# Sums that end token half by token half, a shorter root, and a norm folded into the next one's weights

## The reference

```python
def rms_norm(x, g):
    y = xf * lax.rsqrt(jnp.mean(xf * xf, axis=-1, keepdims=True) + RMS_EPS)
    return (y * g.astype(jnp.float32)).astype(x.dtype)
def swiglu(x, w_gu, w_down):
    gate, up = jnp.split(x @ w_gu, 2, axis=-1)
    return (jax.nn.silu(gate) * up) @ w_down
# first_block
    h = h + merged @ w_out[l]                                  # stage "out"
    h = h + peer(rmsnorm(h, norm2_w[l]), ...)                  # "wq", "pu", "pv"
    return rmsnorm(h, final_norm_w)
# second_block
    x = x + 0.5 * rms_norm(swiglu(rms_norm(x, ffn1_pre_g[l]), ...), ffn1_post_g[l])   # "gu1", "dn1"
    y = hybrid_mixer(rms_norm(x, mix_pre_g[l]), ...)                                  # "in2" ... "wo"
    x = x + rms_norm(y, mix_post_g[l])
    x = x + 0.5 * rms_norm(swiglu(rms_norm(x, ffn2_pre_g[l]), ...), ffn2_post_g[l])   # "gu2", "dn2"
```

## Time and profile before

| | us |
|---|---|
| median of 3 runs | 1586.11 (1584.76 to 1589.0) |
| profiled execution | 1585.57 |
| its span | 1584.0 |
| TensorE busy, matmul | 1502.1 (95%) |
| VectorE busy | 1117.8 (71%) |
| ScalarE busy | 732.2 (46%) |
| GpSimd busy | 272.1 (17%) |

### The profile page before, as it was taken

How to read it: one execution, slowest core, us unless ns; L and a number is a source line. 1 busy time by engine, 2 the same in 40 slices (tenths; PEclk the granted TensorE clock), 3 DMA queues, 4 the chain that set the end, 5 groups by cost and what they waited for, 6 DMA issues and landing times.

```text
span 1584.0 us, 27622 instructions
## 1 busy us (share of the span) xinstructions
PE 1502.1 (95%) x10710; PEld 1381.2 (87%) x10710; DVE 1117.8 (71%) x1590; ACT 732.2 (46%) x835; POOL 272.1 (17%) x306
## 2 busy tenths in 40 slices
PE   7999998999999999999999999989999886699997
PEld 7989897999999999998888888879998785599975
DVE  5557666699999898657676676667773665677743
ACT  4356653545454444444444444444433455244431
POOL 1100000000000111136556545500000100000000
PEclk9999999999999999999999999999999995899999
DMA  7643334476665877788888877745555440335551
GB/s 256 217 160 135 130 141 166 154 246 233 238 230 206 279 262 267 250 306 293 289 304 279 287 291 297 284 146 194 204 185 185 135 173 1 133 137 209 187 184 53
DMA packets 56291, 329.66 MB, mean 208 GB/s; under 512 B 7472, under 2 KB 7520, under 8 KB 24720
## 3 DMA queue, kind: packets, MB, share of 16 engines
q1 hardware_dynamic: 35856, 259.01, 46.2%
q0 software_dynamic: 20352, 69.47, 12.7%
HBM read 294.90 MB, written 33.55 MB: 207 GB/s over the span
## 4 chain that ended last, share of the span: by engine, by line
PE 84%; DVE 10%; ACT 4%; DMA 1%; issue 1%; DVEq 0%; SPq 0%; ACTq 0%
PE ub L1535 14%; PE ub L1536 14%; PE ub L1537 14%; PE acc L1535 11%; PE acc L1537 11%; PE acc L1536 11%; DVE wl L878 3%; PE acc L1729 3%; DMA raw<-in_wstream 1%; ACT wh L528 1%; PE acc L1600 1%; PE mb L1625 1%; PE acc L1499 1%; PE mb L1610 0%; DVE esel L1231 0%
## 5 line engine op out<-in xcount | busy, mean ns | idle before, releaser
L878 DVE TENSOR_TENSOR wl<-raw,wh 128x2048 fp32r<-128x2048 f32 x245 | 582.6, 2379 | 300.2 <-ACT wh L528 298.9
L1535 PE MATMUL ub<-xh,wh 128*128 128x256 f32 x2216 | 622.5, 281 | 6.6 <-DVE wl L878 5.8
L528 ACT CAST wh<-raw 128x2048 fp32r<-128x2048 f32 x245 | 467.9, 1910 | 337.0 <-DMA raw<-in_wstream 239.7
L1536 PE MATMUL ub<-xl,wh 128*128 128x256 f32 x2216 | 615.3, 278 | 0.0
L1537 PE MATMUL ub<-xh,wl 128*128 128x256 f32 x2216 | 615.2, 278 | 0.0
L1535 PEld LDWEIGHTS ub<-xh,wh 128*128 128x128 f32 x2216 | 417.3, 188 | 13.7 <-DVE wl L878 7.1
L1536 PEld LDWEIGHTS ub<-xl,wh 128*128 128x128 f32 x2216 | 418.1, 189 | 0.1
L1537 PEld LDWEIGHTS ub<-xh,wl 128*128 128x128 f32 x2216 | 418.1, 189 | 0.0
L1535 PE MATMUL acc<-wh,ah 128*128 128x512 f32 x512 | 199.2, 389 | 0.5 <-issue 0.5
L1537 PE MATMUL acc<-wh,al 128*128 128x512 f32 x512 | 199.2, 389 | 0.0
L1536 PE MATMUL acc<-wl,ah 128*128 128x512 f32 x512 | 199.2, 389 | 0.0
(11 more groups left out here) (309 smaller groups left out, 1641.4 us busy)
## 6 DMA issues: line engine op xcount, KB each, us to landing
raw<-in_wstream SPq DMA_DIRECT2D x245, 1024.0 KB, 4.9
gates<-gst POOLq DMA_DIRECT2D x16, 1024.0 KB, 15.4
gl_in<-gates POOLq DMA_DIRECT2D x64, 256.0 KB, 4.9
hidden<-hid POOLq DMA_DIRECT2D x60, 256.0 KB, 5.1
hid<-hidden POOLq DMA_DIRECT2D x60, 256.0 KB, 4.8
resid<-in_x SPq DMA_DIRECT2D x2, 512.0 KB, 3.9
rb<-in_rel POOLq DMA_DIRECT2D x1, 1024.0 KB, 8.1
wb<-in_ffn_post_g POOLq DMA_DIRECT2D x2, 512.0 KB, 3.8
```

The source lines that it names most:

```text
L528: act.copy(wh[:, slot, :], raw[:, slot % RAW, :]).then_inc(w_high, 1)
L878: v.tensor_tensor(wl[:, slot, :], raw[:, slot % RAW, :], wh[:, slot, :].bitcast(F32), ALU.subtract).then_inc(w_low, 1)
L1535: pe.matmul(dst, sh, mh, start=first, stop=False)
L1536: pe.matmul(dst, sh, ml, start=False, stop=False)
```

## The change

1. In the five acc stages the last two chunks are one tail (`acc_tail`): its matmuls go bank by bank, 12 each, for both chunks. The semaphore `a_half` rises after token half 0 and again after bank 2, `c_done` by two at the end. The tail starts when both chunks, and in `pv` both steps' `al`, are there. Additions, squares and roots go by half 0, bank 2 and bank 3. The preparation of the chunk that `ahead` gave after the last chunk of an acc stage is moved behind `normed` of the next stage.
2. The root has two steps in place of three: after the first guess 7 instructions stood for 9, with constants that give the root times a factor `ROOT`, which the mean's factor takes out again. A factor of 0.5 or 1-LAM_INIT goes into the mean as well.
3. After `pv` the transposes take the bare sum. `final_norm_w` is multiplied into the columns of the next norm's weights (`fcol`), `y_again` holds `resid * wb`, and both means and roots are computed together on four columns (`two_roots`). `resid` is scaled after unit 0 (`first_scaled`).
4. The row for the scaling is made between the two tiles of unit 1 (`split_unit`), no longer ahead of it. Transposed blocks lie in `mb`, `ub` and the banks 0 and 1 of `acc`.
5. The output leaves in three copies. `shift_y`, a tile without use, is 8 columns smaller and `fcol` takes that place.

```diff
-            return (acc[:, k, 0:T] if k < 4 else mb[:, k - 4, 0:T] if k < 6 else
-                    ub[:, 1 - u % 2, (k - 6) * T:(k - 5) * T])
+            bank = (mb[:, 0, :], mb[:, 1, :], ub[:, 1 - u % 2, :], acc[:, 0, :], acc[:, 1, :])
+            at = k % 2 * T if k >= 2 else 0
+            return bank[k if k < 2 else k // 2 + 1][:, at:at + T]
...
-            for tt in range(TT):
-                sp.wait_ge(r_ok, LAST_R + tt + 1)
-                sp.dma_start(out[tt * P:tt * P + P, :], resid[:, tt, :]).then_inc(x_out, 16)
+            for n, (tt, lo, hi) in enumerate(((0, 0, D), (1, 0, HALF), (1, HALF, D))):
+                sp.wait_ge(r_ok, R_OF["dn2"] + n + 1)
+                sp.dma_start(out[tt * P:tt * P + P, lo:hi], resid[:, tt, lo:hi]).then_inc(x_out, 16)
...
+            pool.dma_start(fcol[:, :], A["fcol"]).then_inc(par1, 16)
...
-            def square_acc(scratch):
-
-                square(acc_of(0), scratch, 0)
-                halves[0] += 1
-                act.wait_ge(half_ok, halves[0])
-                square(acc_of(1), scratch, 1)
+            def square_acc(stage, scratch):
+
+                h = 2 * TAILS.index(stage)
+                act.wait_ge(a_half, h + 1)
+                square(acc_of(0), scratch, 0)
+                act.wait_ge(a_half, h + 2)
+                square(acc[:, 2, :], scratch, 1)
+                act.wait_ge(c_done, CH[stage] + dict(_sizes)[stage])
+                square(acc[:, 3, :], scratch, 2)
...
                 normed(w, UN[gu])
-                square_resid(junk_again, 1)
+                square_resid(stage, 1, junk_again)
+                if stage == "pv":
+                    act.wait_ge(t_ok, 2)
+                    square(y_again[:, 1, :], junk_again, 3, ROOT / 32.0)
                 C, U = CH[gu], UN[gu]
+                ahead(C - 1)
...
-                for _ in range(3):
-                    link(v.tensor_tensor(ta, dst, dst, ALU.mult))
-                    link(v.scalar_tensor_tensor(tb, ta, -0.5, src, ALU.mult, ALU.mult))
-                    link(v.scalar_tensor_tensor(dst, tb, 1.5, dst, ALU.add, ALU.mult))
+                guess(dst, src, ti)
+                link(v.tensor_tensor(tb, dst, dst, ALU.mult))
+                link(v.tensor_tensor(ta, tb, src, ALU.mult))
+                link(v.scalar_tensor_tensor(tb, ta, 10.0 / 3.0, ta, ALU.subtract, ALU.mult))
+                link(v.scalar_tensor_tensor(dst, tb, 5.0, dst, ALU.add, ALU.mult))
+                link(v.tensor_tensor(tb, dst, dst, ALU.mult))
+                link(v.tensor_tensor(ta, tb, src, ALU.mult))
+                link(v.scalar_tensor_tensor(dst, ta, 64.0 / 3.0, dst, ALU.subtract, ALU.mult))
+
+            def root(lo, hi):
...
+                    for t in range(lo, hi):
+                        x, z = var[:, t:t + 1], rstd[:, t:t + 1]
+                        ins = v.scalar_tensor_tensor(nw_a[:, t:t + 1], z, x, z, ALU.mult, ALU.mult)
+                    link(ins)
...
-                v.wait_ge(c_done, CH[stage] + dict(_sizes)[stage])
-                weighted(scratch)
-                if factor != 1.0:
-                    link(v.tensor_scalar(rstd[:, :], rstd[:, :], factor, None, ALU.mult))
-                for tt in range(TT):
-                    next_resid(v.scalar_tensor_tensor(resid[:, tt, :], scratch[:, tt, :], rstd[:, tt:tt + 1],
-                                                      resid[:, tt, :], ALU.mult, ALU.add))
+                weights()
+                squares(1)
+                link(v.tensor_tensor(scratch[:, 0, :], acc_of(0), wb[:, :], ALU.mult))
+                mean(0, 1, factor=factor)
+                root(0, 1)
+                squares(1)
+                v.tensor_tensor(scratch[:, 1, half(0)], acc[:, 2, :], wb[:, half(0)], ALU.mult)
+                next_resid(v.scalar_tensor_tensor(resid[:, 0, :], scratch[:, 0, :], rstd[:, 0:1],
+                                                  resid[:, 0, :], ALU.mult, ALU.add))
+                squares(1)
+                v.tensor_tensor(scratch[:, 1, half(1)], acc[:, 3, :], wb[:, half(1)], ALU.mult).then_inc(wb_used, 1)
+                both_halves()
+                mean(1, 2, factor=factor)
+                root(1, 2)
+                for n in range(2):
+                    next_resid(v.scalar_tensor_tensor(resid[:, 1, half(n)], scratch[:, 1, half(n)], rstd[:, 1:2],
+                                                      resid[:, 1, half(n)], ALU.mult, ALU.add))
...
+            add_first("out")
+            add_half("out", 0)
+            squares(1)
+            mean(0, 1)
+            root(0, 1)
+            add_half("out", 1)
+            v.tensor_scalar(y[:, 0, :], resid[:, 0, :], rstd[:, 0:1], None, ALU.mult).then_inc(t_in, 1)
...
-            add_acc("pv")
-            rstd_ready()
...
+            def first_norm():
+
+                add_first("pv")
+                weights()
+                v.wait_ge(r_ok, nr[0])
+                weigh(0)
+                add_half("pv", 0)
+                add_half("pv", 1)
+
+            def two_roots():
+
+                v.wait_ge(r_ok, nr[0])
+                weigh(1)
+                v.engine_nop().then_inc(wb_used, 1)
+                squares(4)
+                k = ROOT ** 2
+                link(v.tensor_scalar(var[:, 0:2], ssq[:, 0:2], k / D, k * EPS, ALU.mult, ALU.add))
+                link(v.scalar_tensor_tensor(var[:, 2:4], var[:, 0:2], EPS, ssq[:, 2:4], ALU.mult, ALU.add))
+                root(0, 4)
+                spread_root(2)
...
+            def split_unit(c, u):
+
+                pe.wait_ge(w_low, c + 1)
+                pe.wait_ge(u_free, u + 1)
+                unit_tile(c % RING, u % 2, 0)
+                scale_row()
+                unit_tile(c % RING, u % 2, 1).then_inc(c_done, 1)
...
+            def acc_tail(c, cmod, halves, beside=None):
+
+                pe.wait_ge(w_low, c + 2)
...
+                part(0, 0)
+                part(0, 1).then_inc(a_half, 1)
+                part(1, 0).then_inc(a_half, 1)
+                if beside is not None:
+                    beside()
+                part(1, 1).then_inc(c_done, 2)
...
+            for j in range(2):
+                value_step(15, j)
+            pe.wait_ge(a_l, 64)
+            acc_tail(CV + 62, CV + 62, [(ah[:, j, :, :], al[:, j, :, :]) for j in range(2)],
+                     beside=lambda: turn_resid("pv", UN["gu1"], tts=(0,)))
```

316 lines of the change are left out of this document (185 added, 131 removed).

## The result

The changed kernel took 1576.1 us in the median of 5 runs (1571.84 to 1577.83) beside 1586.11 us (1582.82 to 1589.0) for the kernel before: ratio 0.9925, 95% interval 0.9903 to 0.9948. Two later groups of 6 runs each, on another occasion each, gave medians of 1568.44 and 1569.59 us, with ratios 0.9886 (0.9859 to 0.9912) and 0.9904 (0.9874 to 0.9934). The mean of the three ratios, 0.9905, is 15 us. The forecast was 1564.2 us in a range of 1559 to 1572, a gain of 21.9. The direction was right and the size too large: 15 us of 21.9 arrived (12 us in the first group), and the first median lies above the range.

What follows compares the result with a forecast made beforehand. TensorE's matmuls bound the kernel, busy 1502 of 1584.0 us, so only idle time could be won. Gains 4.6 + 4.1 + 4.1 + 5.2 + 3.0 + 0.9 = 21.9 us off 1586.11 gave 1564.2, range 1559 to 1572.

Steps and rivals of the forecast that it cites:

- rival 2: At three joints the clock returns late, counted from unit 0's first matmul: some 5 us lost, 1569.2 us; chance 0.12.
- Rival 3: The clock holds through the gaps broken up by transposes: 2.4 us more gain, 1561.8 us; chance 0.13.
- out's low half: At out to wq, a low half ending at 252.70 delays the first addition, so the chain starts 1.8 us late.
- dn1 to in2: Joint from stage dn1 to in2: early work on token halves brings unit 1 forward, gain 4.1 us.
- rival 1: Restarts starve on longer loads: unit 3 waits 1.7 us longer after pv, 1.4 after dn1 and wo; 1568.7 us; chance 0.19.
- the wide root: In the mixer, 9 steps instead of 11 after the mean, each 0.46 us, ahead of a waiting TensorE: gain 0.9 us.
- the tail of pv: Before pv's last two chunks, 62 and 63, TensorE waits 1.7 us for both low parts of the gated hidden values.
- waits at units 2 and 3: In gu1 after pv, VectorE's two low halves delay scaling: a stall of about 2 us at unit 2, 1 at unit 3.
- out and wo: Joints out to wq and wo to gu2: unit 1 starts earlier, gains of 4.6 and 5.2 us.
- The chain of a joint: At dn1 and wo, TensorE transposes the second token half from about 4 us after the last matmul's end, T.
- The end: Program end: last quarter in place 4.5 us after the last matmul; output copy's price left as before; gain 3.0 us.
- rival 4: Token halves don't come early because casts and low halves are queued; only end and wide root gain: 1582.2 us; chance 0.05.

Runs made afterwards that it cites:

- filled joints: Changed kernel plus matmuls with unread results in the idle stretches ahead of wq, in2 and gu2: 1568.91 us, 0.9882 of the kernel before.
- the earlier cast and low half: Changed kernel with the extra chunk's cast and low half moved earlier behind dn1 and wo: 1574.29 us, 0.9919 of the kernel before.
- scaling first: Changed kernel with VectorE scaling ahead of the low half for the first two units of gu1, gu2 and in2: 1575.85 us, 0.9935 of the kernel before.

## Why the prediction was wrong

**Wrong: the clock.** The forecast let the clock come back in the new joints as in the old ones, and rival 2, with 12 in 100, said that it would come late. Read from windows of half a us, it came back at S+10.3 to 13.8 in the 20 joints of before, while unit 0 started at S+10.1 to 12.5: by half of that time at half clock, in the mean 0.5 us a joint were lost. In the changed kernel it fell at S+3.3 to 5.8 in all nine joints at out, dn1 and wo and came back at S+7.4 to 10.9, while unit 0 starts at S+6.0 to 7.4: 1.4 us a joint in the mean, up to 2.0. The step that failed is the assumption that the clock's return moves forward as far as the work does. At out, dn1 and wo unit 0 moved forward by 3.7, 4.1 and 5.2 us in the mean, the return by 1.7, 2.5 and 3.0. By the filled joints that took about 1 us from out and 0.6 to 0.8 from dn1 and wo each. Rival 2's mechanism was right, its 5 us too much: about 2.5. Rival 3, a clock that holds through broken gaps, is out: eight transposes in the gap don't hold it. The rule that I cited (the Trainium skill, TensorE: Matmul & The Clock Gate, Part 4: PE-mode transpose) is not borne out in its strict form: in the kernel before the clock came back at S+10.3 after out, with transposes alone since S+7.4, and in three of its 20 joints it was back ahead of unit 0. Nor did the fall stay as long as it was: at out, dn1 and wo the clock stood at 0.50 for 7.5 us in the mean before and for 4.6 in the changed kernel. That unit 0 would pay for the return did come true: 2.7 us of those 4.6 lay behind its start, 0.8 of the 7.5 before.

**Wrong: out's low half.** The first addition was to begin at 252.70, S−3.3, from the low half's end in a single trace. It began at S−2.8 to −2.2 in the three traces of the changed kernel (S−4.0 to −2.2 over these and the nine kernels built on it), since the load ahead of it comes when it comes. In the mean of the three that is 0.7 us of the 1.7 missing at out; the clock is the rest.

**Wrong: dn1 to in2,** the largest loss, 3.3 us of 6.4 by the table, of which 0.8 are the clock's by the filled joints. Unit 1 stood at S+12.2 to 13.5, forecast S+12.4. The step that failed is the statement that units 2 and 3 are hidden "with next to nothing to spare": unit 3 waited 1.0 and 0.6 us in the second and third trace (in the first unit 0 had run at half clock for so long that it found its data). That is what rival 1 said of this place (1.4 us). More than that, I had followed the chain only to unit 3, while in2 has VectorE work in every unit (convolutions, the softplus steps) and no slack to catch up: a gain of 3.8 us at unit 1 is 3.0 at unit 3 and 1.6 at the scores. The late work on the extra chunk, and the loads asked for late by it, are the larger part of the cause (the earlier cast and low half brought 1.7 us at the scores, in one trace). That VectorE's amount of work per unit is another fits with scaling first, which only moved the wait, but no run takes work away from it. Between scores and wo 0.1 to 0.2 us of the wide root's 0.9 arrived in the mean, since the wait of 1.1 to 1.9 us in front of the scores made the clock fall at the gates in two of three executions: from the scores to wo it is 51.3 and 50.3 us there and 50.0 in the third, against 50.2 to 51.0 before. How much of the rest belongs to which is open.

**Size only: the tail of pv.** 1.7 us were forecast for the wait ahead of it, and 1.5, 2.5 and 3.1 came, the last with a loss of 1.6 us to the half clock behind it. The row from which I took the cast's start was one in which no load was late; ScalarE's cast waits over 2 us (up to 5.1) in 19 to 54 of some 63 steps of this loop, by execution (eight traces of the two kernels), nearly always for a load. A bound from a single row should have carried a range. The other terms of the joint were right: waits at units 2 and 3 of 1.5 to 1.8 and 0.9 to 1.0 us (2.1 and 1.1), and 5.2 us for the rest against 5.8.

**Right.** out and wo with the clock held, and at out with the low half where the prediction had it: 4.8 and 5.1 us (4.6 and 5.2). The chain of a joint, step by step: second half's transposes at T+4.0. The end, 3.6 against 3.0: from the end of the last residual to the end of the span it is 2.5 us and was 3.2, and the half as large output copy, which I had left at its old price, is the likely reason, not tested. That the early halves and not the root carry the gain (rival 4 was wrong). That VectorE's two low halves would hold up gu1's units 2 and 3, and that gu1 and gu2 don't starve beyond that for longer loads (rival 1; in2 does at unit 3): in gu1 unit 4 and later follow at 5.44 to 5.6 us.

**The range.** It was made of the terms' bounds and left out what an execution does by itself. The terms missed 6.4 us, and the first group of runs lay another 5 above the two later ones.
